# Expert weights of a mixture-of-experts layer: six pieces of 2 MB on two queues become twelve of 1 MB on one

## The reference

```python
def expert_block(args):
    tok, e = args
    xb = xt[tok]
    h = jax.nn.silu(xb @ w_gate[e]) * (xb @ w_up[e])
    return h @ w_down[e]
...
out = jax.ops.segment_sum(y, row_tok, num_segments=t)
```

## Time and profile before

| | |
|---|---|
| median of 3 runs | 1432.5 us (1431.42 to 1433.8) |
| span of the profiled execution, first to last instruction | 1429.4 us |
| mean granted TensorE clock | 0.936 of full speed |
| TensorE busy with matmuls | 1154.3 us (81%) |
| VectorE, ScalarE, GpSimd busy | 354.6, 264.3, 39.4 us |
| DMA | 479.99 MB, mean 336 GB/s |

### The profile page before, as it was taken

One profiled execution on the slowest core, in us unless ns is written; L12 is line 12 of the kernel. 1 busy time (PEld: TensorE's weight loads), 2 busy tenths in 40 slices (PEclk: granted clock), 3 DMA queues, 4 the chain that ended last, 5 costly groups with the idle time before them and its releaser, 6 DMA issues.

```text
span 1429.4 us, 14971 instructions
## 1 busy us (share of the span) xinstructions
PE 1154.3 (81%) x5810; PEld 635.7 (44%) x5810; DVE 354.6 (25%) x620; ACT 264.3 (18%) x333; POOL 39.4 (3%) x57
## 2 busy tenths in 40 slices
PE   5999999989858876878878778777788787887880
PEld 5999989878735322222222222222222222222220
DVE  5365959645355000000000000000000000000004
ACT  5433444453322100010000100000000001000011
POOL 1000000000000000000000000000000000000001
PEclk9999999999969999999899989999989999989995
DMA  7555454456422999999999999999999999999964
GB/s 280 192 187 177 163 188 143 165 202 231 171 92 115 430 428 428 427 428 428 427 429 427 428 416 428 425 428 426 416 427 423 427 428 423 426 425 428 427 294 181
DMA packets 66223, 479.99 MB, mean 336 GB/s; under 512 B 8303, under 2 KB 8303, under 8 KB 40724
## 3 DMA queue, kind: packets, MB, share of 16 engines
q1 hardware_dynamic: 47620, 276.17, 48.0%
q10 hardware_dynamic: 13392, 195.04, 32.1%
q0 software_dynamic: 5184, 8.40, 1.6%
HBM read 473.29 MB, written 18.87 MB: 344 GB/s over the span
## 4 chain that ended last, share of the span: by engine, by line
DMA 47%; PE 47%; DVE 2%; issue 2%; ACT 1%; DVEq 0%; ACTq 0%; SPq 0%; POOLq 0%; POOL 0%
DMA ring<-in_w_up 45%; PE bank L1091 23%; PE bank L1247 18%; PE bank L1248 1%; PE bank L1267 1%; DMA stage<-in_w_in 1%; DMA ring<-y_sorted,slot_i 1%; PE bank L1233 1%; PE bank L1234 1%; PE bank L1070 1%; PE bank L1200 0%; DVE zone_u L751 0%; ACT w_hi L305 0%; PE bank L1168 0%; DVE x_tok L1047 0%
## 5 line engine op out<-in xcount | busy, mean ns | idle before, releaser
L1247 PE MATMUL bank<-ring,spare 128*64 128x512 f32 x1024 | 482.1, 627 | 117.4 <-DMA ring<-in_w_up 114.4
L1248 PE MATMUL bank<-ring,spare 128*64 128x512 f32 x1024 | 483.5, 628 | 0.0
L1247 PEld LDWEIGHTS bank<-ring,spare 128*64 128x64 f32 x1024 | 143.0, 144 | 426.6 <-issue 426.6
L1267 PE MATMUL bank<-ring,spare 128*64 128x512 f32 x1024 | 247.6, 640 | 16.5 <-DVE spare L1017 16.5
L1015 DVE TENSOR_TENSOR hidden<-silu_g,bank 64x512 f32<-64x512 f32 x32 | 22.1, 690 | 600.0 <-ACT silu_g L656 600.0
L1091 PE MATMUL bank<-h_hi,w_hi 128*128 128x256 f32 x576 | 163.5, 284 | 1.5 <-DVE w_lo L311 1.5
L1091 PE MATMUL bank<-h_lo,w_hi 128*128 128x256 f32 x576 | 163.1, 283 | 0.0
L1091 PE MATMUL bank<-h_hi,w_lo 128*128 128x256 f32 x576 | 163.1, 283 | 0.0
L311 DVE TENSOR_TENSOR w_lo<-stage,w_hi 128x2048 fp32r<-128x2048 f32 x60 | 137.0, 2290 | 98.2 <-ACT w_hi L305 97.9
L1267 PEld LDWEIGHTS bank<-ring,spare 128*64 128x64 f32 x1024 | 75.4, 147 | 165.1 <-issue 144.0
L1248 PEld LDWEIGHTS bank<-ring,spare 128*64 128x64 f32 x1024 | 143.0, 144 | 0.0
(11 more groups left out here) (220 smaller groups left out, 733.0 us busy)
## 6 DMA issues: line engine op xcount, KB each, us to landing
ring<-in_w_gate SPq DMA_DIRECT2D x64, 2048.0 KB, 19.1
ring<-in_w_up ACTq DMA_DIRECT2D x62, 2048.0 KB, 22.6
ring<-in_w_down SPq DMA_DIRECT2D x33, 2048.0 KB, 20.8
ring<-in_w_down ACTq DMA_DIRECT2D x31, 2048.0 KB, 20.6
stage<-in_w_in SPq DMA_DIRECT2D x44, 1024.0 KB, 4.9
stage<-in_w_out SPq DMA_DIRECT2D x16, 1024.0 KB, 5.1
ring<-in_w_up SPq DMA_DIRECT2D x2, 2048.0 KB, 13.5
x_tok<-in_x SPq DMA_DIRECT2D x2, 1024.0 KB, 5.9
```

Of the source, the lines that this page charges most:

```text
L1247: M.matmul(bank[0][0:W_ROWS, :], win[:, c, :], ring[2 * half][:, at], start=(c == 0), stop=(c == C - 1))
L1248: ins = M.matmul(bank[0][UPPER, :], win[:, c, :], ring[2 * half + 1][:, at], start=(c == 0), stop=(c == C - 1))
L1267: ins = M.matmul(bank[4 + n][upper * W_ROWS:(upper + 1) * W_ROWS, :], hiddenT[:, j * W_ROWS:(j + 1) * W_ROWS], ring[4 + half][:, at:at + N ...
```

## The change

The ring has twelve buffers of 1 MB in place of six of 2 MB: four quarters of gate and of up, in turn, then four quarters of down. SyncE begins them all, in the order in which TensorE uses them; ScalarE begins none. `in_used` goes up four times per expert and `down_used` four times, and TensorE waits for two pieces before each quarter of gate and up, and for one before each quarter of down. `gathered_rows` uses four whole buffers. The diff, with the quantities that count experts in ScalarE's and VectorE's functions:

```diff
--- before.py
+++ after.py
@@ -40,8 +40,9 @@
 N_HALVES = N_HEADS // HALF_HEADS
 OUT_BLOCK0 = N_FIRST + 3 * N_HALVES
 MOE_BLOCK0 = OUT_BLOCK0 + D // NB
-PIECES = 6
-PIECE = C * NB // 2
+QUARTERS = 4
+PIECES = 2 * QUARTERS + J
+PIECE = C * NB // QUARTERS
 assert MOE_BLOCK0 % 3 == 0 and PARTS == 3 and C % STAGES == 0
 
 
@@ -284,8 +285,8 @@
 
             gate, up, down = (a[n][0][bass.ds(e, 1)].rearrange("e (p x) n -> p (e x n)", p=P)
                               for n in ("w_gate", "w_up", "w_down"))
-            first, second = slice(0, PIECE), slice(PIECE, 2 * PIECE)
-            return [gate[:, first], up[:, first], gate[:, second], up[:, second], down[:, first], down[:, second]]
+            quarter = [slice(q * PIECE, (q + 1) * PIECE) for q in range(QUARTERS)]
+            return [w[:, at] for at in quarter for w in (gate, up)] + [down[:, at] for at in quarter]
 
         def load(sp, b, chunks):
 
@@ -316,7 +317,7 @@
 
 
         def gathered_rows(k, t):
-            return ring[k][:, t * D:(t + 1) * D]
+            return ring[2 * k + t][:, :]
 
         SCORE_BANK, TURN_BANK, OUT_BANK = (6, 7, 0, 1), (2, 3, 6, 7), (4, 5, 0, 1)
 
@@ -345,31 +346,22 @@
             def load_piece(k, src):
                 sp.dma_start(ring[k][:, :], src).then_inc(piece_loaded[k], 16)
 
-            def load_even_pieces(t, e):
-
-                pieces = expert_pieces(e)
-                sp.wait_ge(in_used, 2 * t - 1)
-                load_piece(0, pieces[0])
-                sp.wait_ge(in_used, 2 * t)
-                load_piece(2, pieces[2])
-                sp.wait_ge(down_used, 2 * t - 1)
-                load_piece(4, pieces[4])
-
             first_pieces = expert_pieces(0)
             for b in range(D // NB):
                 load(sp, OUT_BLOCK0 + b, columns(w_out, b * NB))
                 if b == 1:
 
                     sp.wait_ge(used, chunk(4 * OUT_BLOCK0 - 1))
-                    load_piece(0, first_pieces[0])
-                    load_piece(1, first_pieces[1])
-
-            sp.wait_ge(lo_made, chunk(4 * MOE_BLOCK0 - 1))
-            load_piece(2, first_pieces[2])
-            load_piece(3, first_pieces[3])
+                    for k in range(4):
+                        load_piece(k, first_pieces[k])
+
+            for k in range(4, 8):
+
+                sp.wait_ge(lo_made, chunk(4 * (MOE_BLOCK0 - 1) + k - 4))
+                load_piece(k, first_pieces[k])
             sp.wait_ge(used, chunk(4 * MOE_BLOCK0 - 1))
-            load_piece(4, first_pieces[4])
-            load_piece(5, first_pieces[5])
+            for k in range(8, PIECES):
+                load_piece(k, first_pieces[k])
 
             sp.wait_ge(sorted_done, C)
             sp.dma_start(final_w[:, :], a["final_g"].rearrange("(o d) -> o d", o=1).broadcast_to([P, D])).then_inc(fg_loaded, 16)
@@ -377,14 +369,15 @@
             def load_expert(t, e):
 
                 for k, src in enumerate(expert_pieces(e)):
-                    if k in (0, 2):
-                        sp.wait_ge(in_used, 2 * t + (k // 2 - 1))
-                    if k >= 4:
-                        sp.wait_ge(down_used, 2 * t + (k - 5))
+                    if k < 2 * QUARTERS:
+                        if k % 2 == 0:
+                            sp.wait_ge(in_used, QUARTERS * t + (k // 2 + 1 - QUARTERS))
+                    else:
+                        sp.wait_ge(down_used, J * t + (k - 2 * QUARTERS + 1 - J))
                     load_piece(k, src)
 
             with sp.Fori(1, E) as e:
-                load_even_pieces(e, e)
+                load_expert(e, e)
 
             sp.wait_ge(tables_ready, 1)
             flag = sp.value_load(over_i[0:1, OVER:OVER + 1], min_val=0, max_val=E)
@@ -642,22 +635,12 @@
                 first = act.value_load(start_i[0:1, bass.ds(t, 1)], min_val=0, max_val=SLOTS)
                 nc.scalar.activation(win, x_sorted_from(first), ACT.Copy).then_inc(win_ready, 1)
 
-            def load_odd(k, t):
-                act.dma_start(ring[k][:, :], expert_pieces(t)[k]).then_inc(piece_loaded[k], 16)
-
-            def expert_act(t, loads_next):
-
-                if loads_next:
-                    act.wait_ge(in_used, 2 * t + 1)
-                    load_odd(1, t + 1)
-                act.wait_ge(in_used, 2 * t + 2)
-                if loads_next:
-                    load_odd(3, t + 1)
+            def expert_act(t):
+
+                act.wait_ge(in_used, QUARTERS * t + QUARTERS)
                 nc.scalar.activation(silu_g[UPPER, :], bank[0][0:W_ROWS, :], ACT.Silu).then_inc(silu_done, 1)
                 window(t + 1)
-                act.wait_ge(down_used, 2 * t + 2)
-                if loads_next:
-                    load_odd(5, t + 1)
+                act.wait_ge(down_used, J * t + J)
                 act.wait_ge(rows_free, t + 1)
                 nc.scalar.activation(y_rows[:, 0:NB], bank[4][:, :], ACT.Copy).then_inc(y_act, 1)
 
@@ -666,16 +649,15 @@
             act.wait_ge(sorted_act, C // 2)
             act.wait_ge(sorted_dve, C // 2)
             window(0)
-            expert_act(0, True)
+            expert_act(0)
             act.wait_ge(tables_ready, 1)
-            with act.Fori(1, E - 1) as e:
-                expert_act(e, True)
-            expert_act(E - 1, False)
+            with act.Fori(1, E) as e:
+                expert_act(e)
             nc.scalar.activation(warm[:, :], warm[:, :], ACT.Sqrt)
             flag = act.value_load(over_i[0:1, OVER:OVER + 1], min_val=0, max_val=E)
             with act.If(flag > 0):
                 with act.Fori(E, E + OVER) as t:
-                    expert_act(t, False)
+                    expert_act(t)
                 nc.scalar.activation(warm[:, :], warm[:, :], ACT.Sqrt)
 
             for t in range(T):
@@ -1017,7 +999,7 @@
                 V.tensor_copy(hiddenT, bank[2][:, 0:J * W_ROWS]).then_inc(hiddenT_ready, 1)
                 dve.wait_ge(rows_free, t + 1)
                 V.tensor_copy(row_now[:, :], row_i[:, bass.ds(t, 1)]).then_inc(row_ready, 1)
-                dve.wait_ge(down_used, 2 * t + 2)
+                dve.wait_ge(down_used, J * t + J)
                 V.tensor_copy(y_rows[:, NB:HD], bank[5][:, :]).then_inc(y_dve, 1)
 
             dve.sem_inc(y_dve, 1)
@@ -1239,13 +1221,13 @@
             def expert_pe(t):
 
                 pe.wait_ge(win_ready, t + 1)
-                for half in range(2):
-                    pe.wait_ge(piece_loaded[2 * half], 16 * t + 16)
-                    pe.wait_ge(piece_loaded[2 * half + 1], 16 * t + 16)
-                    for i in range(C // 2):
-                        c, at = half * (C // 2) + i, slice(i * NB, (i + 1) * NB)
-                        M.matmul(bank[0][0:W_ROWS, :], win[:, c, :], ring[2 * half][:, at], start=(c == 0), stop=(c == C - 1))
-                        ins = M.matmul(bank[0][UPPER, :], win[:, c, :], ring[2 * half + 1][:, at],
+                for q in range(QUARTERS):
+                    pe.wait_ge(piece_loaded[2 * q], 16 * t + 16)
+                    pe.wait_ge(piece_loaded[2 * q + 1], 16 * t + 16)
+                    for i in range(C // QUARTERS):
+                        c, at = q * (C // QUARTERS) + i, slice(i * NB, (i + 1) * NB)
+                        M.matmul(bank[0][0:W_ROWS, :], win[:, c, :], ring[2 * q][:, at], start=(c == 0), stop=(c == C - 1))
+                        ins = M.matmul(bank[0][UPPER, :], win[:, c, :], ring[2 * q + 1][:, at],
                                        start=(c == 0), stop=(c == C - 1))
                     ins.then_inc(in_used, 1)
                 pe.wait_ge(hidden_ready, t + 1)
@@ -1257,16 +1239,14 @@
                 pe.wait_ge(hiddenT_ready, t + 1)
                 pe.wait_ge(y_act, t + 1)
                 pe.wait_ge(y_dve, t + 1)
-                for half in range(2):
-                    pe.wait_ge(piece_loaded[4 + half], 16 * t + 16)
-                    for i in range(J // 2):
-                        j = half * (J // 2) + i
-                        for n in range(2):
-                            for upper in range(2):
-                                at = i * D + (2 * upper + n) * NB
-                                ins = M.matmul(bank[4 + n][upper * W_ROWS:(upper + 1) * W_ROWS, :],
-                                               hiddenT[:, j * W_ROWS:(j + 1) * W_ROWS], ring[4 + half][:, at:at + NB],
-                                               start=(j == 0), stop=(j == J - 1))
+                for j in range(J):
+                    pe.wait_ge(piece_loaded[2 * QUARTERS + j], 16 * t + 16)
+                    for n in range(2):
+                        for upper in range(2):
+                            at = (2 * upper + n) * NB
+                            ins = M.matmul(bank[4 + n][upper * W_ROWS:(upper + 1) * W_ROWS, :],
+                                           hiddenT[:, j * W_ROWS:(j + 1) * W_ROWS], ring[2 * QUARTERS + j][:, at:at + NB],
+                                           start=(j == 0), stop=(j == J - 1))
```

## The result

| | before | changed |
|---|---|---|
| median | 1433.15 us (1431.42 to 1436.3, 6 runs) | 1439.76 us (1437.92 to 1440.21, 6 runs) |
| span of the profiled execution | 1429.4 us | 1438.3 us |

The ratio is 1.0039, with a 95% interval of 1.0027 to 1.0051: the change makes the kernel slower by 0.4%, 5.6 us by the ratio and 6.6 us between the medians, where 0.4% faster was forecast. The profiled spans differ by 8.9 us. A run's whole time is 1.9 us over its span in the changed kernel, so the profiled execution of before took about 1431.3 us, near the fast end of its runs.

A forecast was written before the change was run, and what follows sets the result against it. The prediction took the stage as bound by DMA bytes of experts 1 to 31. Its terms, -3.5 - 6.0 + 7.4 + 1 - 4.6 = -5.7 us, took 1432.5 to 1426.8 us, range 1420 to 1438.

The forecast's parts named there:

- The bound: Expert stage: bound by the bytes of experts 1 to 31, 390 MB, some 920 us, with the DMA engines full.
- Start of the stream: Expert 1's first loads go out after a quarter of gate and up instead of a half: -3.5 us.
- End of the stream: Last expert: TensorE needs 3.5 us after the last byte instead of 9.5, by finer pieces in order of use: -6.0 us.
- Packets: Whole stream: 8 KB runs add 1488 packets per DMA engine at 5 ns each: +7.4 us.
- (b): Whole stream, slower: 8 KB packets cost what their rows say; 1435.6 us at 10.9 ns, about 1452 at 414 GB/s; chance 0.12.
- One queue: Whole stream: SyncE's queue alone moves 0.5% more than two queues together: -4.6 us.
- Transfers: Whole stream: 186 more transfers, each with a completion on all 16 engines: +1 us.
- (a): Ends give less: the slowest engine's lag grows by half, 3.7 us come back, 1430.5 us; chance 0.18 together with (d).
- (c): Whole stream, slower: a single queue leaves a gap after each transfer; 1445.4 us at 50 ns each; chance 0.06.
- (d): End of the stream: pieces do not land in order of use, the 6.0 us vanish, 1432.8 us; chance 0.18 with (a).

The follow-up runs named there:

- quarters at the ends: One-queue kernel with 2 MB pieces, but expert 1's gate and up and the last expert's second half of them in 1 MB quarters: 1423.54 us against 1433.87 before.
- the even and odd partitions: Kernel before, each 2 MB piece loaded by two 1 MB transfers, of even and of odd partitions, 16 KB runs: 1433.8 us against 1433.87, ratio 1.0004.

## Why the prediction was wrong, point by point

The profiles divide each kernel's time into three parts: from TensorE's first matmul of the stage to the first load of expert 1, from there to the end of the last packet of weights (the stream), and from there to the end of TensorE's last down. In us:

| kernel | runs | first load after | stream | last down after |
|---|---|---|---|---|
| before | 16 KB | 7.1 | 931.9 | 9.2 |
| one queue, 2 MB | 16 KB | 7.3 | 931.8 | 9.3 |
| quarters at the ends | 16 KB | 3.7 | 932.2 | 5.9 |
| changed, two profiles | 8 KB | 3.8, 3.8 | 946.9, 946.3 | 5.5, 5.8 |
| two queues, 1 MB, two profiles | 8 KB | 3.7, 3.7 | 946.5, 945.7 | 5.3, 5.6 |
| 2 MB in runs of 8 KB | 8 KB | 7.1 | 946.1 | 12.7 |
| 2 MB in runs of 4 KB | 4 and 16 KB | 7.1 | 959.2 | 9.6 |

The stream's length goes by the length of the runs alone: neither the size of the pieces nor the number of queues moves it by more than about 1 us.

**The bound.** Right. The stage is bound by the bytes of experts 1 to 31; every run that lengthened the stream lengthened the time by about as much.

**Start of the stream, -3.5 us.** Right: 3.8 us from TensorE's start to the first load instead of 7.1, a gain of 3.3.

**End of the stream, -6.0 us.** Right in mechanism, too large in size. It took 5.5 us from the last packet to the end of down, not 9.2 as before and not the 3.5 of the forecast: a gain of 3.7. The last wait for a quarter ended 9.4 us before the last packet, near the 9.8 forecast. 1.4 of the missing 2.3 us are down at the lower clock, 8.53 against 7.09 us; I had priced such a fall at 1.7 us and left it out, and the quarter waits of 1.3 to 1.9 us did not prevent it. Both ends together gained 3.3 + 3.7 = 7.0 us in the changed kernel, and as much with quarters at the ends alone against the one-queue kernel; the forecast was 9.5.

**Packets, +7.4 us: the step that failed.** I took 5 ns for each of 1488 packets, between 0 and 10.9, by subtracting from the line through 2 KB and 16 KB packets what records overlap. Runs of 8 KB alone cost 13.4 us, 9.0 ns each, and runs of 4 KB 8.3 ns each; by the streams they cost 14.2 us and 27.3 us, 9.5 and 9.2 ns each. The subtraction was the error: the line itself, 10.9, was near. The two short stretches with 8 KB runs, which gave 33 us, overstated it more than the line. At 9.0 ns the step is above the 8.8 ns that I had worked out as the point from which the change loses, but that point leaned on two gains that were not there in full. With ends of 7.0 us and a queue worth nothing it is 7.0 / 1488 = 4.7 ns, and at my own 5 ns the change would already have gained nothing. So the rival (b) has the right mechanism, and even its 1435.6, at 10.9 ns, lies 4.2 us under the measured 1439.8, since it counts the same two gains.

**One queue, -4.6 us: the second step that failed.** I read 0.5% better from stretches of 5 us with a share rounded to 0.01. With 2 MB pieces the stream is as long with one queue as with two (931.8 and 931.9 us); at 1 MB the medians agree within 0.1 us.

**Transfers, +1 us.** Between 0 and 2.4 us: the even and odd partitions took the same time with a stream 2.4 us longer, and the changed kernel's stream is 0.2 to 0.8 us longer than that of 2 MB pieces in runs of 8 KB.

Put together from the two profiles: +15.0 for the stream, where the forecast had +3.8 for packets, transfers and queue; -3.3 and -3.7 for the ends, where it had -9.5. That is +8.0 against -5.7. So packets were the largest error, but not all that was wrong, as I had thought after the result. The expert stage also began 1.2 us later (450.02 against 448.79), and what follows down took 0.4 us less, which makes 8.8 of the 8.9 us between the spans. The medians lie 6.6 us apart, and 4.7 (1438.78 against 1434.09) when run again. The 1 to 3 us between these and the profiles are not settled. The form with two queues came out 3.1 us over before the first time and 4.7 the second, and its two profiles began the expert stage at 448.31 and 450.20, so the part ahead of the stage scatters by about as much.

**Rivals.** (a) foresaw that the engines would run apart, and they do, over 18 us where it was 7. It put this down to the order of a single queue, but with two queues and 1 MB pieces they thin out over 17 us too (1382 to 1399). With 8 KB packets in 2 MB pieces the stream was as long and the transfers ended closer together, 352 GB/s at 1394 to 1396 and 29 at 1400 to 1402:

```profile
1394.00:1396.00 2.00, 2.00 (x8) 0.84 (x10) 0.00 (x0) 0.00 (x0) 0.00 (x0) 0.79 0.85 352
...
1400.00:1402.00 2.00, 2.00 (x12) 0.86 (x10) 0.00 (x0) 0.00 (x0) 0.00 (x0) 1.00 0.07 29
```

The slowest engine ended at nearly the same time there (1401.5), so the wide spread is the fast ones running ahead into the freer ring, and costs nothing by itself; that is argued from these two traces, not tried. (c), a gap after each transfer, is excluded by the even and odd partitions for two queues, and by the equal pair above for one. (d) did not occur.

The overhead of about 3 cycles per packet in the Trainium skill, "DMA: Bandwidth & Descriptors", Why small descriptors are slow, gives an estimate of 5.4 us for the packets. The runs here show 13.4 us by the times and 14.2 by the streams, so for packets of 8 KB, which the section does not treat as small, it is too low by more than half; the measurement decides. The figure of the same page of the Trainium skill, Measured, 341 GB/s for 1 MB in transfers begun by GpSimd, does not hold for the queued transfers of SyncE here: 422 GB/s.

## What to carry to other kernels

When a kernel is bound by DMA at full share, what counts is nanoseconds per packet: multiply the added packets of one engine by the price before cutting pieces finer, and take the price from a line through packet sizes in the trace without discounting it (10.9 ns by the line, 8.3 to 9.5 measured). Small pieces pay only where the stream starts and ends, so cut those alone: with one queue in order of use that gained 10.3 us here, some 7 of them at the ends by the profiles, where cutting all of it lost 5 to 7. A share that is already 1.01 can't show a loss; GB/s at that share does.

## What the runs showed of the hardware that was not expected

A 1 MB load of partitions 0 to 63 or 64 to 127 in 16 KB runs streams at 229 to 234 GB/s, at a DMA share of 1.01, and the same load of every second partition at 428. The Trainium skill, "DMA: Bandwidth & Descriptors", Rules for kernel authors, advises against disjoint partition halves, as they share the same engines, but the trace shows more than that: nearly half the rate is lost. The scatter to `y_sorted`, which nothing changed, lands in a median of 15.0 us before and 7.9 in the changed kernel; with one queue and 2 MB pieces it is 10.1, with two queues and 1 MB pieces 10.2. So one loading queue in place of two shortens it both times. Shorter packets do not always: with two queues and 2 MB pieces it is 10.6 in runs of 8 KB, but 14.1 with gate and up in runs of 4 KB. What sets it is open. It costs nothing here, since the next scatter is 30 us away.
